# Wide operand tiles on multiples of 512 bytes, an earlier threshold for the pair behind a down product, and two queue orders

## What is computed

```python
for layer in range(2):
    y = conv_lru_mixer(x, ...) if layer == 0 else diff_attention_mixer(x, ...)
    x = layer_norm(DN_ALPHA * x + y, mix_ln_g[layer], mix_ln_b[layer])
    x = layer_norm(DN_ALPHA * x + swiglu(x, w_gate, w_up, w_down), ffn_ln_g[layer], ffn_ln_b[layer])
...
def swiglu(x, w_gate, w_up, w_down):
    return (jax.nn.silu(x @ w_gate) * (x @ w_up)) @ w_down
```

## Time and profile before

| | before |
|---|---|
| median of 3 executions | 3579.5 us (3579.48 to 3579.87) |
| the profiled execution | 3579.45 us, of which the span from first to last instruction 3577.7 us |
| TensorE busy | 3481.6 us (97%) in 15,838 matmuls |
| VectorE, ScalarE, GpSimd busy | 1966.8 us (55%), 1327.5 us (37%), 669.0 us (19%) |
| mean granted TensorE clock | 0.988 of 2.4 GHz |
| DMA | 258.89 MB, mean 72 GB/s |

### The profile page before, as it was taken

The page is one execution under the profiler, slowest core; times in us unless marked ns, Lnnn a source line. Parts: engine busy times, 40 slices in busy tenths (PEclk is TensorE's granted clock), DMA queues, the critical chain, the costliest instruction groups (busy, mean ns, idle before and its releaser), DMA issues. The chain is left out here.

```text
span 3577.7 us, 41727 instructions
## 1 busy us (share of the span) xinstructions
PE 3481.6 (97%) x15838; PEld 2784.3 (78%) x15838; DVE 1966.8 (55%) x2572; ACT 1327.5 (37%) x2008; POOL 669.0 (19%) x398
## 2 busy tenths in 40 slices
PE   9999999999999999989999999999999899999998
PEld 7768877777877777768888888888876778888886
DVE  7986556665476565667323233554567764323235
ACT  4444432323354444455311112445453442212133
POOL 0007332111261000013000000354124430000014
PEclk9999999999999999999999999999999999999999
DMA  3102222231132111122222123233331222111112
GB/s 104 38 29 89 86 76 80 83 95 65 56 98 70 42 47 29 52 60 77 83 76 89 52 93 105 91 95 90 104 94 52 69 89 88 47 47 47 47 59 100
DMA packets 82680, 258.89 MB, mean 72 GB/s; under 512 B 10352, under 2 KB 17904, under 8 KB 82544
## 3 DMA queue, kind: packets, MB, share of 16 engines
q1 hardware_dynamic: 82544, 257.07, 23.6%
HBM read 243.92 MB, written 4.72 MB: 69 GB/s over the span
## 5 line engine op out<-in xcount | busy, mean ns | idle before, releaser
L202 PE MATMUL ps<-xh,whi 128*128 128x512 f32 x2136 | 764.6, 394 | 15.2 <-POOL xl L500 9.9
L202 PE MATMUL ps<-xl,whi 128*128 128x512 f32 x2136 | 756.7, 391 | 0.0
L202 PE MATMUL ps<-xh,wlo 128*128 128x512 f32 x2136 | 756.5, 391 | 0.0
L178 ACT ACTIVATE whi<-stage 128x1024 fp32r<-128x1024 f32 (+1 forms) x316 | 330.4, 1046 | 854.9 <-PE ps L202 825.8
L185 DVE TENSOR_TENSOR wlo<-stage,whi 128x1024 fp32r<-128x1024 f32 (+1 forms) x316 | 458.4, 1451 | 325.7 <-ACT whi L178 324.4
L202 PEld LDWEIGHTS ps<-xh,whi 128*128 128x128 f32 x2136 | 402.8, 189 | 108.4 <-POOL xl L500 9.8
L202 PEld LDWEIGHTS ps<-xh,wlo 128*128 128x128 f32 x2136 | 403.0, 189 | 85.0
L202 PEld LDWEIGHTS ps<-xl,whi 128*128 128x128 f32 x2136 | 403.4, 189 | 82.8
L202 PE MATMUL ps<-hh,whi 128*128 128x512 f32 x864 | 301.4, 395 | 2.1 <-DVE hl L3514 1.7
L202 PE MATMUL ps<-hh,wlo 128*128 128x512 f32 x864 | 300.9, 394 | 0.0
L202 PE MATMUL ps<-hl,whi 128*128 128x512 f32 x864 | 300.8, 394 | 0.0
(11 more groups left out here) (536 smaller groups left out, 5925.8 us busy)
## 6 DMA issues: line engine op xcount, KB each, us to landing
stage<-in_w_ff SPq DMA_DIRECT2D x88, 512.0 KB, 3.7
stage<-in_w_gate SPq DMA_DIRECT2D x59, 512.0 KB, 3.6
stage<-in_w_up SPq DMA_DIRECT2D x59, 512.0 KB, 3.6
stage<-in_w_in SPq DMA_DIRECT2D x50, 512.0 KB, 3.6
ada<-in_w_ada SPq DMA_DIRECT2D x48, 512.0 KB, 3.8
stage<-in_w_qkv SPq DMA_DIRECT2D x43, 512.0 KB, 3.6
stage<-in_w_out SPq DMA_DIRECT2D x24, 512.0 KB, 3.6
stage<-in_w_down SPq DMA_DIRECT2D x24, 448.0 KB, 3.3
```

Of the source, the lines that this page charges most:

```text
L178: act.activation(whi[slot][:, wide(g, k)], stage[slot][:, wide(g, k)], ACT.Copy).then_inc(w_hi, 1)
L202: done = pe.matmul(acc[:, h * HALF:(h + 1) * HALF], wt[slot][:, w], xt[:, b, h * HALF:(h + 1) * HALF], start=b == 0 and wt is whi and xt i ...
```

## The change

1. *Addresses.* to_line pads up to the next multiple of 512 bytes. It is called ahead of x and ahead of REGION; mod and moments now lie ahead of x, and the unused tiles mv, sd and rstd are gone. x begins at 16,896 = 33 x 512, xh at 49,664, xl at 82,432, stage at 115,200 and 119,296, whi at 123,392 and 127,488, wlo at 131,584 and 135,680, REGION at 142,336 = 278 x 512: all wide tiles have 0 bytes over. The sizes of the matmuls and their order on PE are as before.
2. *The pair that opens a group* (p = 2, 4, ... 12) waits for 6 of the 8 adds of the down product ahead of it instead of for all 8.
3. *ACT and DVE in the early down product:* t4h and t4l of block b go into unit b + 3 instead of b + 2.
4. *DVE at its end:* the first two weight parts of the first pair are split ahead of the residual of the last unit instead of behind it.

```diff
--- before.py
+++ after.py
@@ -76,6 +76,17 @@
     def sem(name):
         return ctx.enter_context(nc.semaphore(name))
 
+    LINE = 512
+
+    def to_line(name):
+        at = -(-nc.sbuf_base // 32) * 32
+        if at % LINE:
+            sb(name, [P, (LINE - at % LINE) // 4])
+        return nc.sbuf_base
+
+    mod = sb("mod", [P, NMOD, DB])
+    moments = sb("moments", [P, 2, 24])
+    to_line("pad_x")
     x = sb("x", [P, DB, S])
     XH_AT = nc.sbuf_base
     xh = sb("xh", [P, DB, S], F32R)
@@ -90,18 +101,13 @@
     ident = sb("ident", [P, P])
     one = sb("one", [P, 1])
     share = sb("share", [P, 2])
-    mv = sb("mv", [P, 2, 2])
     stats = sb("stats", [P, 2, 2, 6])
-    sd = sb("sd", [P, 2, 1])
-    rstd = sb("rstd", [P, 2, 1])
     eps = sb("eps", [P, 1])
     credit = sb("credit", [P, 9])
     ps = [ctx.enter_context(nc.psum_tensor(f"ps{k}", [P, S], F32)) for k in range(4)]
-    mod = sb("mod", [P, NMOD, DB])
     gb2 = sb("gb2", [P, DB])
     ada_sum = sb("ada_sum", [P, 2])
     lam_t = sb("lam_t", [P, 8])
-    moments = sb("moments", [P, 2, 24])
     mx = sb("mx", [P, 2, 2])
     nb = sb("nb", [P, 2, 2])
     den = sb("den", [P, 2, 2])
@@ -112,7 +118,7 @@
         return cols[:, at + k:at + k + 1] if isinstance(k, int) else cols[:, bass.ds(k + at, 1)]
 
     ones = one[:].to_broadcast([P, P])
-    REGION = -(-nc.sbuf_base // 32) * 32
+    REGION = to_line("pad_region")
 
     def at_kb(name, shape, kb, dtype=F32):
 
@@ -1591,8 +1597,8 @@
                 split_hi(act, f_e, 0, u + 1)
             if u < HB:
                 cross_t1_act(act, u)
-            if 2 <= u < 2 + HB:
-                cross_t4_act(act, u - 2)
+            if 3 <= u < 3 + HB:
+                cross_t4_act(act, u - 3)
             if u == 4:
                 act.wait_ge(lam_mm, 1)
                 act.activation(lam_t[:, 2:4], ps[2][:, 0:2], ACT.Exp).then_inc(lam_e, 1)
@@ -1642,11 +1648,14 @@
                 split_lo(dve, f_e, 0, u + 1)
             if u < HB:
                 cross_t1_dve(dve, u)
-            if 2 <= u < 2 + HB:
-                cross_t4_dve(dve, u - 2)
+            if 3 <= u < 3 + HB:
+                cross_t4_dve(dve, u - 3)
+            if u + 1 == DB:
+                part_lo(dve, 0, 0)
+                part_lo(dve, 0, 1)
             residual(dve, f_e, u, ALPHA)
-        for n in range(4):
-            part_lo(dve, 0, n)
+        part_lo(dve, 0, 2)
+        part_lo(dve, 0, 3)
         m = 0
         for p in range(FAST_PAIRS):
             final = p == FAST_PAIRS - 1
@@ -1711,7 +1720,10 @@
         opens, closes = (0, 1, 3), (1, 5, 6)
         if p >= 2:
             pe.wait_ge(*s_h.at(2 * p - 2))
-            pe.wait_ge(*dn_out.at(DB * min(p // 2, FAST_GROUPS)))
+            if opens_group(p):
+                pe.wait_ge(*dn_out.at(DB * (p // 2 - 1) + DB - 2))
+            else:
+                pe.wait_ge(*dn_out.at(DB * min(p // 2, FAST_GROUPS)))
         if p == 1:
             pe.wait_ge(acc_free, gf.base + 2)
         for n in range(7):
```

## The result

The changed kernel takes 3536.4 us (median of 4 runs, 3533.17 to 3538.17) against 3579.5 us of the kernel before (4 runs, 3576.18 to 3579.87): a ratio of 0.9881, 95% interval 0.9863 to 0.9898. It is 43 us faster. The forecast was 178 us faster (3401, range 3365 to 3480). The profiled execution of the changed kernel took 3538.17 us with a span of 3536.4.

The account below looks back on a forecast made before the run. PE was taken to bound most stages, through the distance between wide matmuls and then its waits. Alignment 163 + opening pair 9.2 + ACT's queue 3.6 + DVE's queue 2 = 178 us off 3579.5, giving 3401 us, range 3365 to 3480.

Parts of the forecast that it names:

- the 99 us of the xh family: Alignment gain for 8,496 wide matmuls, mainly xh and xl moving: 226.7 to 215 ns, 11.7 ns each, before losses.
- the first term: Alignment of all wide operands: matmul distance falls to 215 ns, 178 us less 15 of losses, so 163 us.
- The second to fourth: Terms for the opening pair (9.2 us), ACT's queue (3.6 us) and DVE's queue (2 us).
- B: Rival: only part of the surcharge goes, 220 ns left, or other engines become the limit; 3461 us; chance 0.10.
- C: Rival: tile contents or writers set the two paces, so only the three waits count; 3564 us; chance 0.08.
- D: Theory from the experiments, not the prediction: the moving operand's start less the weights' start decides the matmul pace.
- D of the prediction: Rival: surcharge is 64 cycles less a quarter of the offset, so aligned starts take 240 ns; 3706 us; chance 0.06.
- A: The prediction's main case: alignment and the three waits gain as summed, 3365 to 3435 us; chance 0.74.
- The losses taken off: Gain other engines hide: 5 us from 0 to 250 us, 3 in attention heads, 7 around norms and 2600 to 2900.
- The opening pair: At six group ends PE waits for unit 7's dn_out; waiting for fewer adds gains 9.2 us.
- ACT's and DVE's queues: Early down product: t4 one unit later gains 3.6 us; first pair's wlo ahead of the last residual gains 2.
- the half clock: After the wait near 475 us, PE runs 3.4 us at 1.2 GHz: about 8 matmuls, 1.6 us more.

Follow-up runs that it names:

- probe_fine: Changed kernel plus added matmuls at start differences in 16-byte steps and with step-0 operands; no difference below 226.7 ns a matmul, 218.4 with moving step 0.
- probe_grid: Changed kernel plus added matmuls, weights started at 0 to 448 bytes and moving operand at 0 to 192; 226.8, 229.4, 232.3, 233.2 ns by difference.
- all_at_64: Changed kernel with x to wlo and REGION all 64 bytes past a multiple of 512; 3535.65 us, ratio 0.9875 to the kernel before.
- aligned_only: Changed kernel with only the new addresses, the old opening-pair threshold and both old queue orders; 3556.4 us, ratio 0.993 to the kernel before.
- weights_64: Changed kernel with stage, whi and wlo 64 bytes past a multiple of 512, moving operands left on multiples; 3608.3 us, ratio 1.0078 to the kernel before.
- opening_only: Kernel before with only the changed wait threshold of the opening pairs; 3572.0 us, ratio 0.9975.
- probe_all: Changed kernel plus 23 rows of added matmuls varying columns, weight width, starts, step 0, accumulators and float type; 384 columns took 174.1 ns, 256 took 119.7.
- probe_offsets: Changed kernel plus 12 x 16 added matmuls, whi[0] fixed, xh read from twelve starts; 226.7 ns at 0 bytes, 236.7 at 4, 228.7 at 64, 233.3 at 448.

## Why the prediction was wrong, and where it was right

**The step that failed** is "Every wide operand then starts on a block, the waste by that rule is 0, and the distance falls to 213.3 ns". Measured are 226.7. The views were read rightly: both paces, the 13.3 and 20.0 ns over 213.3 and the 427.5 ns at clock 0.50 stand as they were. What failed is the rule put behind them: that each surcharge is a waste of the moving operand's read, that its own start decides it, and that alignment takes it all. Two observed pairs (128 bytes with 13.3 ns, 64 bytes with 20.0) were laid on a rule with blocks of 256 bytes read to their end, and so both surcharges had one cause that alignment would remove. A block of 128 bytes, of which the prediction says that it fits neither, gives the 6.7 ns between the two kinds once 13.3 are allowed to stay; that is T, the next theory, and it failed too. The runs show two surcharges:

- A floor of 13.3 ns a matmul, on each of the 12,792 wide matmuls, which no start tried removed (probe_fine, probe_grid, all_at_64). In the sum it was all of the 99 us of the xh family, of which nothing came, and 11.6 of the 18.3 ns a matmul behind the 79 us of the hh family.
- 6.7 ns more when the moving operand's start lies, modulo 256, 64 bytes below the weights' start. Only the 4,296 had it. The change removes it: 4,296 x 6.7 = 29 us by the paces.

So the first term, forecast at 163 us, is 29 by the paces and measured 23.6 alone (aligned_only, interval 20 to 30). The second to fourth measured 14.8 together, as forecast. The two measured parts make 38.4 of the 43.1 us of the medians; with 29 they make 43.6. (A small slip beside it: the groups of PE also hold 288 matmuls of the xh family that the count of 8,496 leaves out, 3.4 us at 11.7 ns.) That the difference of the starts decides and not either start is shown by weights_64 (the moving operand left in place, 72 us slower) and all_at_64 (each start at 64, nothing lost), and by all 32 pairs of probe_grid. The prediction's "the surcharge is not issue or weight load" fits the probes with narrower weights, but the weights' start counts as much as the moving operand's.

**The rivals.** None gave the time: 3536 lies between B (3461) and C (3564). B has the right sign of error, that only part goes, but by another mechanism and with too large a part. C, "addresses don't matter", is refuted by aligned_only, though by 24 us only. The argument against C, the pace of t, was sound: t lies behind REGION and its weights don't. It fits D as well, and the kernel before had only two values of that difference, as it had only two addresses. D of the prediction (a start on the block costs the most) is refuted by after. With A at 0.74 I took one rule for much surer than two points allow; no rival had the floor as a cost of its own that stays.

**The losses taken off.** 15 us were set aside where DVE, ACT or the norms keep PE waiting. Since the xh family got no faster, most of that never arose: DVE's share in the first 200 us did not near 1. What such a loss looks like is shown by weights_64 the other way round, where 14 of 86 us don't arrive, 8.6 of them in the attention and around the norms beside it.

**The opening pair.** Right: six waits gone, 9.2 us forecast, 8.4 measured alone, no new wait for the fourth slot.

**ACT's and DVE's queues.** Right in size and in the waits: 3.6 + 2 = 5.6 us forecast, 6.5 measured, and whi and wlo of the first pair ready before PE wants them. The 1.6 us put on the half clock were right by luck: opening_only keeps a clock of 1.00 behind the same wait and gains nothing by it, since a wait of 1.79 us for DVE follows. The trace of after shows no bracket at the third slot, so the 0.4 us by which it could have been late came back whole or was not there.

**What stays open.** Why the pace goes by the difference of two starts modulo 256, and what the 13.3 ns are that each wide matmul takes at clock 1.00 above half of its time at 0.50. Step 0 in the moving operand takes 8.4 of them away, so these go with the moving operand; whose the other 5 are is not shown. Nor is it shown which weights' start counts, that of the matmul's own or of the next one's, whose load overlaps it in the trace (before has a load of 0.19 us from 1720.05 on, beside the matmul from 1720.05 to 1720.44): in every run here the two are equal modulo 256. For the 5 us by which aligned_only falls short, the clock is a candidate that is large enough, and no run separates it.

## What to carry to other kernels

Where PE is busy throughout, compare the distance between starts over all the operands of one shape: a difference in it is time, and here it was 6.7 ns on a third of the matmuls. For wide matmuls like these (512 columns of 4 bytes in 227 to 237 ns), put the moving operand and the weights on starts that are equal modulo 256 bytes; which start it is made no difference here (3536.4 us at 0, 3535.65 at 64). Before a stretch at half clock gets a price of its own, look at what PE would wait for next if it were faster. A surcharge that all observed cases share may be a floor: count on removing only the part by which they differ, and try a case with the cause changed before the rest goes into a sum.

## What the runs showed of the hardware that was not expected

- The pace of 512 columns of 4 bytes at a granted clock of 1.00 depends on moving start less weights' start, modulo 256: 226.7 to 228 ns at 0, 229 at 64, 232 to 233 at 128, 233 at 192 (probe_grid and probe_all), 236.5 at 240 (probe_fine) and 236.7 at 4 (probe_offsets). At 252 it is 226.8 again (probe_fine).
- At an equal start 512 columns take 226.7 ns, 13.3 more than the 213.3 that are half of 427 at clock 0.50 (426 with equal starts in aligned_only, 427.5 with unequal ones in the earlier trace rows); 384 and 256 columns take 174.1 and 119.7, 14 and 13 above their share. With a moving operand of step 0 it is 218.4 to 218.8, some 5 above. Plain 4-byte float takes (27.63 - 0.59)/63 = 429.2 ns in probe_all, 2.5 above twice 213.3.
- The same wait of PE is not always followed by the same clock. Behind the 2.0 us at 475 the profiles of before and of aligned_only (2.25 us) have 3.4 us at clock 0.50, and that of opening_only, whose code differs from before only from the third pair on, has 1.00. Behind the 2 us before the first pair, before and opening_only have 1.00 and aligned_only has 3.41 us at 0.50. Each is one profiled execution, so this shows no effect of the addresses.
